# Products of zeros on the tensor engine inside the layer norms of a 2+2-layer model

## What is computed

```
def layer_norm(x, g, b):
    xf = x.astype(jnp.float32)
    mu = jnp.mean(xf, axis=-1, keepdims=True)
    var = jnp.mean(jnp.square(xf - mu), axis=-1, keepdims=True)
    y = (xf - mu) * lax.rsqrt(var + LN_EPS)
    return (y * g.astype(jnp.float32) + b.astype(jnp.float32)).astype(x.dtype)
...
    x = layer_norm(x, emb_ln_g, emb_ln_b)
    for l in range(DEPTH):
        h = hybrid_mixer(x, ...)
        x = layer_norm(alpha * x + h, ln_g[l, 0], ln_b[l, 0])
        h = memory_cross_attention(x, mem, xa_q[l], xa_kv[l], xa_o[l])
        x = layer_norm(alpha * x + h, ln_g[l, 1], ln_b[l, 1])
        h = conv_ffn(x, ffn_w_in[l], ffn_conv_w[l], ffn_conv_b[l], ffn_w_out[l])
        x = layer_norm(alpha * x + h, ln_g[l, 2], ln_b[l, 2])
...
    for l in range(DEPTH):
        h = rmsnorm(x, norm1_w[l]) * (1.0 + sc1) + sh1
        x = x + g1 * hybrid_mixer_2(h, ...)
        h = rmsnorm(x, norm2_w[l]) * (1.0 + sc2) + sh2
        x = x + g2 * (swiglu(h, ...) if l == 0 else moe_swiglu(h, ...))
    return rmsnorm(x, final_norm_w)
```

## Time and profile before

| | us |
|---|---|
| median of 3 runs | 3221.89 |
| lowest and highest | 3221.03, 3222.43 |
| the profiled execution | 3222.36 |
| its span in the trace | 3220.6 |
| mean granted clock of TensorE | 0.953 |
| TensorE busy | 3012.2 (94%) |

### The profile page before, as it was taken

The page is one execution under the profiler, slowest core; times in us unless marked ns, Lnnn a source line. Parts: engine busy times, 40 slices in busy tenths (PEclk is TensorE's granted clock), DMA queues, the critical chain, the costliest instruction groups (busy, mean ns, idle before and its releaser), DMA issues.

```text
span 3220.6 us, 38908 instructions
## 1 busy us (share of the span) xinstructions
PE 3012.2 (94%) x16780; PEld 2719.5 (84%) x16780; DVE 1704.3 (53%) x1841; ACT 1371.6 (43%) x1545; POOL 418.4 (13%) x164
## 2 busy tenths in 40 slices
PE   8997998999999798898979999879999999999997
PEld 7886886998888687898868998768889898899896
DVE  1275213563256312565354442447787777777774
ACT  1075002342057101433222342227676776777674
POOL 1000000001000000000000000003333343443342
PEclk9998998999999899899889999979999999999998
DMA  9484522456467440455204555218999999999994
GB/s 307 135 281 143 190 92 88 158 173 192 144 217 247 137 142 29 157 189 166 94 27 157 179 174 170 76 35 333 349 358 336 351 362 337 350 357 340 365 337 157
DMA packets 392051, 678.85 MB, mean 211 GB/s; under 512 B 17184, under 2 KB 286528, under 8 KB 391744
## 3 DMA queue, kind: packets, MB, share of 16 engines
q1 hardware_dynamic: 389344, 666.82, 59.7%
q0 software_dynamic: 2528, 9.46, 1.0%
HBM read 675.19 MB, written 4.69 MB: 211 GB/s over the span
## 4 chain that ended last, share of the span: by engine, by line
PE 92%; DVE 5%; ACT 2%; issue 1%; DMA 0%; DVEq 0%; SPq 0%; POOL 0%
PE bank L486 90%; PE bank L950 1%; PE bank L584 1%; ACT w_hi L1593 0%; DVE ka L1199 0%; DVE probs L1095 0%; DVE w_lo L1100 0%; DVE peak L1079 0%; DVE gates L1392 0%; DVE work L1056 0%; DVE memT L1423 0%; DVE work L1156 0%; ACT ring_tail L1660 0%; DMA const<-in_const 0%; DVE work L1042 0%
## 5 line engine op out<-in xcount | busy, mean ns | idle before, releaser
L1499 DVE TENSOR_TENSOR ew_lo<-ring_head,ew_hi 128x1792 fp32r<-128x1792 f32 (+1 forms) x288 | 680.8, 2397 | 199.3 <-ACT ew_hi L1786 199.2
L1786 ACT CAST ew_hi<-ring_head 128x1792 fp32r<-128x1792 f32 (+2 forms) x384 | 647.7, 1695 | 274.1 <-PE bank L486 274.1
L468 POOL TENSOR_TENSOR ew_lo<-ring_head,ew_hi 128x1792 fp32r<-128x1792 f32 (+1 forms) x96 | 389.5, 4058 | 1257.3 <-ACT ew_hi L1786 1257.3
L1100 DVE TENSOR_TENSOR w_lo<-ring_head,w_hi 128x2048 fp32r<-128x2048 f32 x108 | 247.6, 2293 | 246.0 <-ACT w_hi L1593 246.0
L1593 ACT CAST w_hi<-ring_head 128x2048 fp32r<-128x2048 f32 x108 | 205.2, 1903 | 327.7 <-PE bank L486 282.7
L486 PE MATMUL bank<-x_hi,w_hi 128*128 128x256 f32 x1152 | 326.4, 291 | 18.9 <-DVE w_lo L1100 12.9
L486 PE MATMUL bank<-x_hi,w_lo 128*128 128x256 f32 x1152 | 322.8, 287 | 0.0
L486 PE MATMUL bank<-x_lo,w_hi 128*128 128x256 f32 x1152 | 321.2, 285 | 0.0
L486 PE MATMUL bank<-ew_hi,xe_hi 128*128 128x448 f32 x1024 | 295.1, 369 | 4.4 <-DVE ew_lo L1499 4.4
L486 PE MATMUL bank<-ew_lo,xe_hi 128*128 128x448 f32 x1024 | 291.5, 366 | 0.0
L486 PE MATMUL bank<-ew_hi,xe_lo 128*128 128x448 f32 x1024 | 291.4, 366 | 0.0
(11 more groups left out here) (328 smaller groups left out, 4513.3 us busy)
## 6 DMA issues: line engine op xcount, KB each, us to landing
ring_head<-in_moe_w_gate SPq DMA_DIRECT2D x128, 896.0 KB, 6.6
ring_head<-in_moe_w_up SPq DMA_DIRECT2D x128, 896.0 KB, 6.9
ring_head<-in_moe_w_down SPq DMA_DIRECT2D x96, 1024.0 KB, 7.0
ring_head<-in_w_in SPq DMA_DIRECT2D x56, 1024.0 KB, 5.9
ring_head<-in_ffn_w_in SPq DMA_DIRECT2D x44, 1024.0 KB, 7.6
ring_head<-in_ada_w SPq DMA_DIRECT2D x32, 1024.0 KB, 8.3
ring_tail<-in_w_in SPq DMA_DIRECT2D x26, 1024.0 KB, 6.5
ring_head<-in_ffn_w_out SPq DMA_DIRECT2D x22, 1024.0 KB, 5.9
```

What stands on the lines that cost most here:

```text
L468: pool.tensor_tensor(ew_lo[:, h, 0:n], ring(c % 6)[:, 0:n], ew_hi[:, h, 0:n].bitcast(F32), ALU.subtract).then_inc(w_used[c % 6], 1)
L1100: v.tensor_tensor(w_lo[:, h, :], ring(s), w_hi[:, h, :].bitcast(F32), ALU.subtract).then_inc(w_used[s], 1)
L1499: v.tensor_tensor(ew_lo[:, h, 0:n], ring(c % 6)[:, 0:n], ew_hi[:, h, 0:n].bitcast(F32), ALU.subtract).then_inc(w_used[c % 6], 1)
L1786: a.copy(ew_hi[:, c % DEPTH_HI, 0:n], ring(c % 6)[:, 0:n]).then_inc(f.count(part_hi), 1)
```

## The change

A function `idle_products(n)` issues n products of the tile `zeros` with itself (a 128x128 part of it as weights, 512 columns moved) into bank 7. They have no wait and set no semaphore. Nothing that the kernel computes reads what they write: bank 7's contents have been read before, and its next use starts over. They stand at three places of a norm: ahead of the variance products (`idle[0]`), between these and the two products that spread the result (3), and behind those (`idle[1]`).

```diff
+            def idle_products(n):
+
+                for _ in range(n):
+                    nc.tensor.matmul(bank[7][:, :], zeros[:, 0:P], zeros[:, :], start=True, stop=True)
+
+            def spread_rstd(idle=0):
+
+                idle_products(3 if idle else 0)
                 pe.wait_ge(inv_ready, f.next(inv_ready))
                 for j in range(2):
                     mm(bank[4][:, TOK + j * P:TOK + (j + 1) * P], std[:, 2 + j:3 + j].to_broadcast([P, P]), ident, True, True,
                        rstd_ready if j else None)
-
-            def norm_var(at=(4, 6)):
+                idle_products(idle)
+
+            def norm_var(at=(4, 6), idle=(5, 8)):
+                idle_products(idle[0])
                 for q in range(4):
                     var_piece(q, at)
-                spread_rstd()
+                spread_rstd(idle[1])
...
-                norm_var((0, 2) if l else (4, 6))
+                norm_var((0, 2) if l else (4, 6), (0 if l else 5, 8))
...
-                spread_rstd()
+                spread_rstd(8)
```

More of the change, by code:

```diff
@@ L564, in var_piece @@
                            var_ready if (t, j) == (KD - 1, 1) else None)
-            def spread_rstd():
+            def idle_products(n):
[3 more added lines that the diff above has]
+                idle_products(3 if idle else 0)
                 pe.wait_ge(inv_ready, f.next(inv_ready))
```

## The result

The changed kernel took **3205.9 us** in the median (3203.9 to 3207.2, 4 runs), the kernel before 3222.2 in the same comparison: a ratio of 0.9943 [0.9928, 0.9957], 16.3 us less. The forecast was 3210.0, with a range of 3201 to 3222. The profiled execution took 3207.16, its span is 3205.3 us, 15.3 less than before, and the mean granted clock rose from 0.953 to 0.962. From that and the span, the time at the low level (2 x (1 - clock) x span) went from 303 us to 244. At the low level a product takes twice as long (0.45 against 0.22 us in the earlier trace rows), so a microsecond there costs half a microsecond at most, and less where TensorE waits anyway: 59 us less gave 15.3, and that includes the price of the added products.

The account below looks back on a forecast made before the run. TensorE, busy 94% of the span, was taken as the bound, slowed by low clock around the norms. Terms -11.0, -1.0, 0, -0.5 and +0.6 sum to -11.9 us, from 3221.9 to 3210.0 us; range 3201 to 3222.

Parts of the forecast that it names:

- Rival 1: At all norms: products of zeros don't hold the clock, only their prices stay; 3241 us, chance 0.12.
- Rival 2: Ahead of the variance products: five are too few, the clock falls where it does now; 3222 us, chance 0.14.
- (a): First four norms: five products ahead keep the clock full through most variance products; -2.0 or -1.8 us each.
- The sign I had named: Third norm's timeline: variance products in 3.6 to 4.6 us instead of 6.16 would show (a).
- N1: The first norm: all steps (a) to (d) together gain there, -3.4 us.
- (b): Between variance products and spreading: the three products stand on the path; +0.5 us at each of the first four norms.
- N8: The eighth norm: three fit the wait, eight cost +1.1, the clock's earlier return gives -1.6; -0.5 us.
- (c): Behind the spreading, first four norms: eight products partly at low clock delay the next stage; 0 to +1.6, taken +0.4 us.
- (d): Stage behind each of the first four norms: the clock returns earlier, while the eight run; -2.3 or -1.2 us.
- I count no loss: Between 25 and 160 us: TensorE paces the stages behind, so they start earlier and gains pass on; nothing deducted.
- N10: The last norm: five change nothing, three cost +0.6, the last eight lie off the path; +0.6 us.
- Rival 3: Mixers' attention, waiting for VectorE: another wait meets part of the gain, half is left; 3216 us, chance 0.09.

Follow-up runs that it names:

- experiment 2: The changed kernel with the tile behind the added products filled with 1.0 instead of 0.0: 3203.6 us, 0.9934 of the kernel before.
- experiment 8: The changed kernel with seven instead of five products ahead of the variance products and none at N10: 3194.9 us (0.991), measured again 3195.2 us (0.9908).
- experiment 6: The changed kernel without the 16 added products at N10: 3206.0 us, 0.9942 of the kernel before.

## Where the prediction was right and where wrong

The total, the sign and the mean clock came out: -16.3 us against -11.9, 0.962 as said. Rival 1 is out: the products of zeros hold the clock, whether they are zeros or ones (experiment 2). The Trainium skill (page "TensorE: Matmul & The Clock Gate", Part 1) says of another throttle, the one on current, that all-zero operands don't trip it; the clock gate makes no such difference here, 0.9934 against 0.9931. Rival 2, "the five are too few", was right in what it says of the five and wrong in the time it gave. The steps:

**(a) The five keep the clock up through the variance products, -2.0 or -1.8 at four norms: wrong in the time, and as a mechanism it holds only at some norms of some executions.** The sign I had named did appear (4.49 us, within 3.6 to 4.6), and it was no proof: at N3 the products take 4.59 with one-column products and 4.77 in the kernel before with a delay, at N2 4.34 with one column against 4.47 after. The 6.16 and 5.81 us of the earlier trace rows, from which I took the gains, hold for one position of the norm against the clock. The faster norms of the other position were paid for between the norms: A is -0.2 for the one-column kernel. The five alone give 0 in the total. In their trace they raise the clock only at N1 (4.04 against 6.41), where nothing is won by it. With the eight behind them there is more. The unchanged program, second trace, at N3:

```profile
763.80 3.73 PE L486 MATMUL bank<-ones,gates 128*128 128x1 f32 x32 [0.36 <-ACT gates L1609]
...
765.10:768.40 3.30, 3.30 (x27) 2.80 (x27) 0.17 (x1) 1.25 (x3) 0.00 (x0) 1.00 1.10 348
768.60:771.80 3.20, 2.98 (x9) 1.21 (x10) 2.79 (x8) 2.41 (x6) 0.00 (x0) 0.50 1.10 348
```

Here the clock stays full through all the variance products, and is low for one short stretch behind them. So it is at N3 in six of the nine traces that have five or seven ahead and the eight; N3 gains 3.5 to 4.1 us in these, 2.6 in the other three and 2.8 with the eight alone. In none of the four traces without moved columns ahead do the products take less than 4.59 there. At N2 no trace shows it (4.37 us at the least), at N4 only the one with seven above. So (a) can be had at N3, for about 1 us instead of 2.0, and depends on the position.

**(b) Three only cost, +0.5 at each norm: likely wrong in sign.** At their own place they cost what I had put: at N3 the spreading begins 1.10 us behind the products instead of 0.55, and at N8 0.8 us later behind the first of them (4.95 against 4.18). What failed is to cost them by their place alone. They close the hole between two stretches of work, and without them C gains 4 us instead of 9.7.

**(c) The eight, +0.4: mis-sized.** From the end of the spreading to the next stage's first product it takes 3.08 us at N3 instead of 2.00, 2.85 at N2 and 2.06 at N4: +1.1, +0.9 and +0.1, within my bounds of 0 and 1.6. The three and the eight together cost 1.4 us at N3: from the first variance product to the next stage's first product it is 9.73 us (767.80 to 777.53) against 8.32 with the five alone (766.48 to 774.80). The price of one was right: 0.23 us at the full level (N4 of experiment 8, 1.60 us for seven), 0.41 at the low one (N8, 1.23 for three).

**(d) The clock returns earlier, -2.3 or -1.2: right as a mechanism, and it carries most of the gain.** The low stretch at N3 is 10.1 us long with the five alone and 6.7 after. The eight alone give 0.27% in the total, where the five alone give nothing, and 11.4 us in A of their trace, where I had 5.4 for (c) and (d) together at four norms. The moment of the return was later than I had it: I expected it at N3 between 774.4 and 776.4, while the eight run, and it came at 777.4, when all eight had run low (3.46 us), so that the price in (c) was nearly the full one.

**The norms singly.** N1: -3.4 forecast, and the next stage started at 26.3 us where before it was 25.8. The step that failed is "I count no loss": the earlier trace rows show TensorE's wait at N1 for ScalarE, 2.0 us, and not that the weights land at nearly the same moment (25.6 us in the trace of before). After:

```profile
22.97 3.30 ACT L1619 ACTIVATE xT<-work,eln 128x256 f32<-128x256 f32 x8 [1.50 <-DVE work L1064]
...
21.81 2.51 PE L569 MATMUL bank<-zeros 128*128 128x512 bf16 x8
26.33 1.07 PE L486 MATMUL bank<-xT,ring_head 128*128 128x256 f32 x2 [2.01 <-issue]
```

ScalarE has begun the eight tiles of the norm at 22.97, 0.4 us each, so that the first piece of two is there at 23.8, and TensorE starts 2.5 us behind it. The profile names no engine for that wait, but it ends with the first chunk of weights, which lands at 26.2 us. The undelayed kernels with five or seven ahead all start there between 25.2 and 26.5 us, each 0.1 us behind that chunk's landing, whenever their norm ends. N2, N3 and N4 gained 2.3, 2.6 and 1.6 us where 2.1, 3.4 and 2.1 were forecast; but the one-column kernel, too, has 1.6 at each. What the zeros add at these three in this trace is 0.7, 1.0 and 0, and 4.7 us more between N3 and N4, in the second layer's attention, where the kernel after wins 3.0 us and the one-column kernel loses 1.7. N5 and N6 gained 1.4 (forecast 1.0), with variance products of 5.33 and 5.38 us, so that N5 lost (4.45 before) and N6 won (6.99). N7 gained 1.5 (forecast a loss of 0.3), N9 0.3 as forecast.

**N8, -4.6 against -0.5,** is the term most mis-sized. Its price was right: the next stage starts 8.05 us behind the first variance product, before 6.88, +1.2 where I had +1.1. Its return wasn't. Before, behind the norm:

```profile
1974.66 6.03 PE L486 MATMUL bank<-work,ring_head 128*16 128x256 f32 x16 [2.00 <-ACT work L1611]
1980.62 4.86 PE L486 MATMUL bank<-ring_head,work 128*128 128x8 f32 x32
```

The first group of 16 took 6.03 us there and takes 3.63 now, the next 4.86, now 3.74, since before the clock fell once more from 1983.1 to 1989.7. I had counted 1.6 us of the 4.8 up to the first return and not looked at what followed it. The second fall isn't there after. Behind N8 another 3.8 us were won in the second mixer (2065 to 2128), for which I had nothing. All traces of kernels with the three and the eight there have it except one (experiment 8, first time). Without the three there are 0.2 and 0.0 with five and eight, and 2.4 with the eight alone, which loses 3.2 again at N9.

**N10, +2.1 against +0.6.** I had put the five into the wait of the earlier trace rows. They stand behind it (experiment 6).

**Rival 3** had its place right: attention ahead of N2 lost 2.8 us. But so it did with one column (2.9) and with a delay (2.8), so it is no answer to the gain.

What stays open: why one program loses 0.3 us between 1560 us and N7 in one trace and 4.3 in another (with seven; 0.2 and 4.2 without the three), beyond that the low stretches lie elsewhere; whether N8's following gain hangs on the three or on the position they bring; and what the five add once the three are there, since the three and the eight were not run without them.

## What to carry to other kernels

Where the clock falls in a chain of short waits, look at its return first. Work ahead of the chain put the fall off only at some norms, and by itself gained nothing in the total; work behind the fall brought the clock back earlier. So fill the waits from the fall to the next stage's first product without a hole, and cost that filling as a whole and not by its pieces. Keep it away from a place that TensorE's own stream reaches late, where it lies on the path. A sign in one trace is no proof of a cause: compare with a kernel that issues the same instructions with next to no work in them, and take more than one trace.

## What the runs showed that I had not expected

The executions of one program differ by more than the effects of single parts. The kernel before took 3220 to 3230.5 us in 55 runs; the traces of one program, changed nowhere up to the cut, have -6.4 and -12.3 us in A. The Trainium skill (page "TensorE: Matmul & The Clock Gate", Part 1) says that the monitor runs freely, so that its phase at a kernel's start, and with it the number of slow products, differs from run to run. These runs agree: the same program has 4.49 us of variance products at N3 in one trace and 3.73 in the next. A delay of 1.8 us at N1 turned the 6.16 us of the kernel before into 4.77, without an edit near them. By that, one trace tells what a place does, and only many runs what the program takes; a part worth 1.8 us (experiment 6) is seen in the first alone.
